# Recurrence of a two-block model: the U factor made by transposing T at each level, factors laid out by head, both directions phase by phase

## The reference

```python
def step(state, inp):
    r_t, w_t, k_t, v_t, kk_t, a_t = inp
    sk = jnp.einsum('bhij,bhj->bhi', state, kk_t)
    state = (state * w_t[:, :, None, :]
             - sk[..., :, None] * (kk_t * a_t)[:, :, None, :]
             + v_t[..., :, None] * k_t[:, :, None, :])
    y = jnp.einsum('bhij,bhj->bhi', state, r_t)
    return state, y
...
for d in range(2):
    ...
    y = y + wkv7_scan(rh, hs(decay), kd, vh, kk, ah, reverse=(d == 1))
```

## Time and profile before

| | us |
|---|---|
| three runs, median | 2842.14 (2839.74 to 2843.65) |
| the profiled execution | 2847.62 |
| its span, first to last instruction | 2845.8 |
| PE busy in the span | 2624.5 (92%) |
| first `turn` of pair 0 to the last `advance` (about 665 to 1120) | about 456 |

### The profile page before, as it was taken

The page is one execution under the profiler, slowest core; times in us unless marked ns, Lnnn a source line. Parts: engine busy times, 40 slices in busy tenths (PEclk is TensorE's granted clock), DMA queues, the critical chain, the costliest instruction groups (busy, mean ns, idle before and its releaser), DMA issues. The chain is left out here.

```text
span 2845.8 us, 54939 instructions
## 1 busy us (share of the span) xinstructions
PE 2624.5 (92%) x23187; PEld 2156.2 (76%) x23187; DVE 1603.1 (56%) x2296; ACT 1137.7 (40%) x1802; POOL 917.4 (32%) x625
## 2 busy tenths in 40 slices
PE   5998999796999998979999999996897999999998
PEld 5776566576889988758888888885776888888887
DVE  7775522467565544666555565445655555556445
ACT  4211332553434332344444443554434444444434
POOL 1302122104112110225777770000412777773000
PEclk9999999898999998989999999998998999999999
DMA  6676433602211221322222227553122322225654
GB/s 232 229 270 214 168 133 155 205 18 80 76 47 48 82 80 32 126 72 76 89 75 81 89 90 276 171 169 109 53 90 73 89 89 74 82 89 216 190 182 144
DMA packets 295927, 346.48 MB, mean 122 GB/s; under 512 B 28383, under 2 KB 224212, under 8 KB 295684
## 3 DMA queue, kind: packets, MB, share of 16 engines
q1 hardware_dynamic: 286044, 336.64, 36.6%
q10 hardware_dynamic: 9640, 6.33, 0.7%
HBM read 271.58 MB, written 71.34 MB: 120 GB/s over the span
## 5 line engine op out<-in xcount | busy, mean ns | idle before, releaser
L2848 POOL TENSOR_TENSOR cg_u_lo<-cg_u_raw,cg_u_hi 128x512 fp32r<-128x512 f32 x210 | 314.9, 1507 | 147.2 <-ACT cg_u_hi L2734 147.2
L131 PE MATMUL cg_ps<-m_hi,cg_u_hi 128*128 128x512 f32 x844 | 331.1, 392 | 25.9 <-DVE cg_u_lo L2923 21.6
L133 PE MATMUL cg_ps<-m_hi,cg_u_lo 128*128 128x512 f32 x844 | 330.3, 391 | 0.0
L132 PE MATMUL cg_ps<-m_lo,cg_u_hi 128*128 128x512 f32 x808 | 315.8, 391 | 0.0
L2734 ACT ACTIVATE cg_u_hi<-cg_u_raw 128x512 fp32r<-128x512 f32 x216 | 132.1, 629 | 380.7 <-PE cg_ps L133 230.0
L131 PEld LDWEIGHTS cg_ps<-m_hi,cg_u_hi 128*128 128x128 f32 x844 | 159.8, 189 | 61.0 <-DVE cg_u_lo L2923 22.4
L131 PE MATMUL cg_ps<-over_y_tx,cg_u_hi 128*128 128x512 f32 x480 | 186.7, 389 | 0.0
L132 PE MATMUL cg_ps<-over_y_tx,cg_u_hi 128*128 128x512 f32 x480 | 186.7, 389 | 0.0
L133 PE MATMUL cg_ps<-over_y_tx,cg_u_lo 128*128 128x512 f32 x480 | 186.7, 389 | 0.0
L133 PEld LDWEIGHTS cg_ps<-m_hi,cg_u_lo 128*128 128x128 f32 x844 | 159.6, 189 | 33.5
L2900 DVE SCALAR_TENSOR_TENSOR cg_z<-cg_ps,top_conv_f,cg_z 128x1023 f32<-128x1023 f32 x88 | 112.9, 1283 | 115.3 <-ACT cg_z L2758 115.3
(11 more groups left out here) (475 smaller groups left out, 6515.2 us busy)
## 6 DMA issues: line engine op xcount, KB each, us to landing
cg_u_raw<-in_ffn_up SPq DMA_DIRECT2D x88, 512.0 KB, 5.1
cg_u_raw<-in_ffn_down SPq DMA_DIRECT2D x64, 512.0 KB, 5.0
qkv_mw<-in_ada_w SPq DMA_DIRECT2D x12, 2048.0 KB
over_f_d_raw<-in_ffn_down SPq DMA_DIRECT2D x48, 512.0 KB, 5.4
scr_act<-cg_z SPq DMA_DIRECT2D x44, 512.0 KB, 2.7
qkv_mw<-in_ada_w SPq DMA_DIRECT2D x8, 1024.0 KB, 11.3
next_w<-in_mix_in SPq DMA_DIRECT2D x16, 512.0 KB, 6.2
za_out<-in_ada_w SPq DMA_DIRECT2D x8, 1024.0 KB
```

Of the source, the lines that this page charges most:

```text
L131: nc.tensor.matmul(out, a_hi, b_hi, start=first, stop=False)
L132: nc.tensor.matmul(out, a_hi, b_lo, start=False, stop=False)
L133: return nc.tensor.matmul(out, a_lo, b_hi, start=False, stop=last)
L2848: G.tensor_tensor(u_lo[:, n % RING], source(g, i), u_hi[:, n % RING].bitcast(F32), ALU.subtract).then_inc(ulo_done, 1)
```

## The change

- U is no longer carried through matmuls of its own. At each level `turn_u` transposes T (at level 0 X1) with four 128x128 transposes per direction, and ACT copies the result (128x512) to `U`. `upper`, `U1` and its filling go. Only after the last level does `last_u` multiply once more; its result goes into the tile T, which `solve` reads.
- X (level_x) leaves PE on the partition half of its head, T comes back on that of its chunk. The outputs spread over two banks (`wide`), and a group of 16 matmuls runs over f, hh, c, so that it visits all four 64x64 tiles.
- On DVE the scans stand behind levels 0 and 1, centring and shift behind levels 2 and 3. `f_edges` (the small products), `f_alphas` and `f_nbetas` of pair m+1 stand behind `carry`, ahead of `advance`. On ACT the exponentials stand behind `solved_z` and `solved_w` of both directions, and the rates behind levels 1 and 2. SP's loads wait one by one for their own buffer.

```diff
-                for u in range(UN):
-                    hh, f = divmod(u, KU)
-                    for c in range(2):
-                        out = bank(g, 3)[side(c), u * HC:(u + 1) * HC].rearrange("p (q b) -> p q b", b=b)
-                        ins = mm(out, xn[g][side(c), hh, 2 * f + c, 0:CH], cols1(src[side(c), u, :], b, 0), start=True, stop=True)
+                for f in range(KU):
+                    for hh in range(2):
+                        for c in range(2):
+                            out = wide(g, 0)[head(hh), slot(f, c), 0:HC].rearrange("p (q b) -> p q b", b=b)
+                            ins = mm(out, xn[g][side(c), hh, 2 * f + c, 0:CH], cols1(src[side(c), pair(f, hh), :], b, 0), start=True, stop=True)
                 ins.then_inc(x_done[g], 1)
...
+            def turn_u(g, m, i):
...
+                src = X1[g] if i == 0 else T[g]
+                for f in range(KU):
+                    ins = nc.tensor.transpose(bank(g, 2)[:, f * P:(f + 1) * P], src[:, 2 * f:2 * f + 2, :].rearrange("p h n -> p (h n)"),
+                                              ident[:, :])
+                ins.then_inc(u_done[g], 1)
...
+            def level_t(g, m, i):
...
+                pe.wait_ge(u_c[g], (NL + 1) * m + i + 1)
                 pe.wait_ge(x_c[g], NL * m + i + 1)
...
+                for f in range(KU):
+                    for hh in range(2):
                         for c in range(2):
...
+                                out = wide(g, 0)[side(c), unit(f, hh), 0:HC].rearrange("p (q b) -> p q b", b=b)
+                                x = cols1(XL[i][g][head(hh), slot(f, c), :], b, 0)
+                            ins = mm(out, U[g][head(hh), slot(f, c), :], x, start=True, stop=True)
+                ins.then_inc(t_done[g], 1)
...
+            def last_u(g, m):
...
+                for f in range(KU):
                     for c in range(2):
+                        for hh in range(2):
+                            ins = mm(wide(g, 1)[side(c), unit(f, hh), 0:CH], XL[NL - 1][g][head(hh), slot(f, c), :], U[g][head(hh), slot(f, c), :],
+                                     start=True, stop=True)
                 ins.then_inc(u_done[g], 1)
...
+            def turn_u(g, m, i):
...
+                act.wait_ge(u_done[g], (NL + 1) * m + i + 1)
+                A(U[g].rearrange("p (c f) n -> p f c n", c=2), bank(g, 2).rearrange("p (f c n) -> p f c n", c=2, n=CH), ACT.Copy).then_inc(u_c[g], 1)
...
+                for g in range(2):
+                    f_exp_in(g, m + 1)
+                    f_exp_before(g, m + 1)
+                    f_exp_out(g, m + 1)
                 for c in range(2):
                     for g in range(2):
                         out(g, m, c)
...
-            def upper(g, m):
-                dve.wait_ge(q_c[g], 4 * m + 4)
-                for c in range(2):
-                    mask = pairs[side(c), 1:2, :].rearrange("p (a b) n -> p a b n", a=1).broadcast_to([CH, 2, KU, CH])
-                    V.copy_predicated(units(U1[g][side(c), :, :]), mask, xn[g][side(c), :, c::2, 0:CH]).then_inc(u1_c[g], 1)
...
                 for g in range(2):
                     carry(g, m)
+                for g in range(2):
+                    f_edges(g, m + 1)
+                    f_alphas(g, m + 1)
+                    f_nbetas(g, m + 1)
                 for c in range(2):
                     for g in range(2):
                         advance(g, m, c)
```

More of the change, by code:

```diff
@@ L1583, in level_tu @@
                 ins.then_inc(u_done[g], 1)
             def solve(g, m):
-                pe.wait_ge(u_c[g], NL * m + NL)
+                if not 0 <= m < NPAIR:
+                    return
+                pe.wait_ge(u_c[g], (NL + 1) * (m + 1))
                 pe.wait_ge(mv_c[g], m + 1)
[L1588 to L1591, removed]
-                                 start=True, stop=True)
+                for f in range(KU):
+                    for hh in range(2):
+                        for c in range(2):
+                            ins = mm(bank(g, 2 + hh)[side(c), f * P:(f + 1) * P], T[g][side(c), pair(f, hh), :], rz[g][side(c), hh * KU + f, :],
+                                     start=True, stop=True)
@@ L1630, in _ @@
             for m in range(NPAIR):
-                for phase in (turn, scores, lower, values):
-                    for g in range(2):
-                        phase(g, m)
+                for g in range(2):
+                    turn(g, m, 0)
+                    turn(g, m, 1)
+                for g in range(2):
+                    scores(g, m, 0)
+                    scores(g, m, 1)
+                for g in range(2):
+                    lower(g, m)
+                for g in range(2):
+                    values(g, m)
                 for i in range(NL):
                     for g in range(2):
+                        turn_u(g, m, i)
                         level_x(g, m, i)
-                    for g in range(2):
-                        level_tu(g, m, i)
-                for phase in (solve, carry):
+                    if i < NL - 1:
+                        for g in range(2):
+                            level_t(g, m, i)
+                for phase in (last_u, solve, carry):
                     for g in range(2):
@@ L1648, in _, with tokens @@
             A = nc.scalar.activation
[L1650 to L1653 removed]
+            def tokens(g, m, part):
+                if not 0 <= m < NPAIR:
+                    return
+                if not 0 <= m < NPAIR:
+                    return
+                if part == 0:
+                    for c in range(2):
+                        act.wait_ge(turned[g], 4 * m + c + 1)
+                        A(xn[g][:, :, c::2, 2 * CH:3 * CH], bank(g, c).rearrange("p (f h e) -> p h f e", f=KU, h=2), ACT.Copy).then_inc(tok_c[g], 1)
+                    return
                 act.wait_ge(turned[g], 4 * m + 3)
@@ L1886, in _ @@
             for g in range(2):
[L1887 removed]
+                for step in (f_edges, f_alphas, f_nbetas):
                     step(g, 0)
@@ L1891, in _ @@
             for m in range(NPAIR):
-                beside(m, 0)
-                for phase in (scores, lower, upper):
-                    for g in range(2):
-                        phase(g, m)
+                for g in range(2):
+                    scores(g, m, 0)
+                    scores(g, m, 1)
+                for g in range(2):
+                    lower(g, m)
                 for i in range(NL):
```

383 lines of the change are left out of this document (264 added, 119 removed).

## The result

The changed kernel took 2798.24 us (median of 4 runs, 2795.36 to 2806.19), the kernel before 2840.94 in the runs beside it (2832.22 to 2843.65). The ratio is 0.9862, with a 95% interval of 0.9844 to 0.9881: by the ratio 39 us less. Forecast were 2807, range 2770 to 2836. The profiled execution took 2795.4 us, with a span of 2793.6, where the sum of the prediction gave 2812.7.

What follows compares the result with a forecast made beforehand. The recurrence was taken as bound by PE's dependent groups in the levels, then a PE, ACT and DVE chain. Terms -64.4 + 4 + 16 + 10.5 - 1 = -34.9 on 2847.6 give 2812.7, less 5.5 profiling excess 2807 us; range 2770 to 2836.

Steps and rivals of the forecast that it cites:

- 64.4 - 4: Levels of all eight pairs: 64.4 us saved, less 4 us added back in case level_t groups are slow.
- The start of the first turn: Ahead of the first kappa: POOL fills two tiles fewer, DVE's own fills then decide, 1 us saved.
- Pace of the groups: PE in the levels: 16 matmuls over four tiles take 0.47 us, not 0.93; for level_t either was possible.
- The 4 us that I added back for level_t: Levels: allowance for level_t, whose rows change only every second matmul; the slow end would be 14 us.
- A level: One level on PE: 3.9 us against 5.58; level 0 4.25, the last level's solve after 4.0.
- Factor work in the levels: DVE work slowed by POOL products: scan behind level 1 adds 0.85 us, centring and shift behind level 2 add 1.45.
- Late state: Behind the carry: contended DVE factor operations make the state 3.1 us late for the third step's closing matmuls, costing 16 us.
- the rival without stops: Behind the carry and in the levels: POOL does not stop DVE, state 0.6 us late; 2770 us, chance 0.12.
- Clock behind the stand: Behind the carry: PE's clock falls after its 3 us stand, 1.5 us a pair, 10.5 us in all.
- Dear tile changes: Levels: PE's tile changes cost 0.35 us each and level_t stays at 0.93; 2835 us, chance 0.14.
- four tiles for nothing: Levels: going round four tiles brings nothing, a level takes 5.4 us; 2844 us, no change, chance 0.06.
- The half clock through the levels: Levels: PE pauses at every evacuation and stays at half clock, a level takes 6.0 us; 2867 us, chance 0.06.

Runs made afterwards that it cites:

- by_head_order: Changed kernel with the loop over heads outermost in a level's products, so a group goes over two array tiles at a time, not four; 25 us slower.
- products_late: Changed kernel with GpSimd's four products of the rates held until VectorE has finished the last level's XL; ratio 0.9784 to the kernel before.
- pool_small: Changed kernel with GpSimd's rho and kappa products cut to four columns from the third pair on; 22 us below the changed kernel by the ratios.
- all_filled: Changed kernel with useless transposes filling TensorE's stands for the late state and for XL in levels 2 and 3; ratio 0.9805 to the kernel before.
- factors_behind: Changed kernel with VectorE's ten factor operations moved from in front of the first chunk's two advances to behind them; 2778.37 us.
- stand_filled: Changed kernel with twenty useless transposes on TensorE where it stands for the late state; ratio 0.9854 to the kernel before.
- levels_filled: factors_behind plus 6 and 12 useless transposes in TensorE's stands at levels 2 and 3, except in the last pair; ratio 0.9811 to the kernel before.

## Why the prediction was right, and where its sizes were off

The profiled execution came out 17 us below the sum. Two terms carry it: the levels gained 7.0 more than 64.4 - 4, and behind the carry 21.0 was lost in place of 26.5. The start of the first turn (5.4 earlier, 1 forecast) is another 4.4, nearly all scatter: the wait before it shrank by 1.2, as forecast.

**Pace of the groups.** Right: 32 records of L1613 in 0.67, two groups of L1644 in 1.13. The 4 us that I added back for level_t were not needed; its rows change only every second matmul, and it keeps the pace of four tiles. by_head_order shows that this pace does hang on the four tiles.

**A level.** 3.70 measured, 3.90 forecast; level 0 took 4.00 (4.25) and the last 3.80 (4.0). I had the pipeline ends and the tile changes a little dear. The scan behind level 0, put at 0.15, did not show. A pair without a fall takes 21.04 in place of 22.4, 9.5 us less over seven. The last took 20.74 in place of 20.0, but 4.00 + 3 x 3.70 + 3.80 is only 18.9: the rest is short pauses, some without a releaser, which no term of the sum had. On top came 5.8 us of clock falls and pauses that the sum did not have: 7 x 21.04 + 20.74 is 168.0, and 173.8 was measured.

**Factor work in the levels.** 0.71 behind level 1 (0.85 forecast) and 1.43 behind level 2 (1.45). products_late confirms that these are GpSimd's doing, but the two waits were not their whole price. They also have a part in the fall of the clock, in the steps as in the levels: without them it fell in one stretch of fifteen instead of eight (products_late). The prediction had that nowhere.

**Late state.** The stand was 2.47 us, 3.1 forecast. The contended chain was right (6.5 us measured, 6.65 stepped through). The 0.6 us between 3.1 and 2.47 are in two halves. The state reached TensorE 0.36 us earlier than stepped through (7.95 behind the first step in place of 8.31). And TensorE came to the closing products 0.3 us later: I wrote 5.2 us behind the first step, where two and a half quarters of 8.64 are 5.4, and it was 5.48. The uncontended state was off for another reason. I added up the lengths of the records, 3.7 us for the ten, but when nothing stops them the small operations start 0.07 to 0.1 us apart and the large ones 0.60, not 0.16 and 0.68, and pool_small runs the ten in 2.98. So the state is in time there and not 0.6 late; the rival without stops would have been worth more than I gave it.

**Clock behind the stand.** 12.66 against 11.17 in the pair without a fall: 1.49 us, 1.5 forecast, in six pairs of the seven. So the late state gave back 3.7 of the 5.5 us and the clock the rest. The size was right and the cause named only half. I wrote that the clock falls because the stand is long. That the stands have to be there is shown by all_filled, where filling them left no fall. But the same 2.5 us stand brings hardly a fall once the two shorter ones in the levels are gone (products_late), and taking the long one away moves the fall to the short ones (factors_behind, stand_filled). And in by_head_order, with less idle time in the levels, the clock fell in seven of eight level stretches. So it is not one stand that costs 1.5 us, and the length of the stands does not decide by itself. I also put the half clock over the next turn. It lies ahead of that, over the last two steps, and is gone at 763.40, before the turn at 763.97.

**The rivals.** Dear tile changes and four tiles for nothing are refuted by the 3.70 us. The half clock through the levels did not come: six of the eight level stretches of the changed kernel are at 0.95 or more. Two have a fall, the longer of them 10.2 us, which made the stretch at 825.92 2.8 us longer. A clock under 1.0 inside the levels was my own sign of being wrong, and in these two it is there. With slower groups in the levels it comes far oftener (by_head_order, seven of eight), so that rival was nearer than its 0.06.

**Still open.** What decides between a fall and none at the same stands is not settled. pool_small stands in the levels exactly as factors_behind does (0.7 and 1.5 us) and has the clock fall in two level stretches of eight, where the other has it in seven. Each count is of one execution. How often the long fall of levels_filled comes was seen in one profile only.

## What to carry to other kernels

Let small matmuls go round all four tiles of the array; here the outputs also lay in two banks, and whether that is needed was not separated. When VectorE and GpSimd both work from SBUF, put their operations at different times: here two moves in the order of work, with no operation removed, brought as much again as the whole change. And judge an edit that is meant to keep TensorE's clock up by stretches, over the whole period of the loop: the clock that one place wins can be lost at the next, and the total then says nothing of the theory.

## What the runs showed of the hardware

Filling TensorE's stands with useless transposes held the clock at 1.00 for 396 us, and the kernel was 16 us faster by the ratios (11.5 by the stretches of the two profiles) than with the stands empty. A copy of 128x4 on VectorE takes 1.25 us beside a GpSimd product and 0.17 alone, so in proportion the smallest operations suffer most. Between the two paces that the prediction knew lies a third. From the first start to the last, a group of 16 matmuls (32 records) takes 0.45 us on four tiles (0.67 with the tail) and 0.70 where the two tiles share a column half (0.92 with it). Where they share a row half and eight matmuls in a row write one bank it takes 0.77 (two groups in 1.76 with the tail). The two diagonal tiles of the kernel before take 0.93. One fall of the clock can last 23.9 us, not only 3.4, 6.8 or 10.2.
